# Second block: gate units between gelu units, a shorter gelu, and the low halves of three weight units with the gating norm's affine part on GpSimd

## The reference

```python
proj = h @ w_in[l]                       # h (256, 1024), w_in (1024, 4296)
q, ckv, qi, ki, wi, u, v, ga, gb = jnp.split(proj, splits, axis=-1)
...
def chunked_gmlp(u, v, ln_g, ln_b, w_s, b_s):
    u = jax.nn.gelu(u)
    v = layer_norm_2(jax.nn.gelu(v), ln_g, ln_b)
...
    s = jnp.einsum('gij,bcjge->bcige', ws, vc) + jnp.transpose(b_s)[None, None, :, :, None]
...
...
merged = jax.nn.sigmoid(ga) * y_a + jax.nn.sigmoid(gb) * y_b
```

## Time and profile before

| | us |
|---|---|
| median of 3 runs | 1447.15 |
| lowest to highest | 1446.86 to 1449.07 |
| the profiled execution | 1444.45 |
| its span in the trace | 1442.7 |

### The profile page before, as it was taken

One profiled execution on the slowest core, in us unless ns is written; L12 is line 12 of the kernel. 1 busy time (PEld: TensorE's weight loads), 2 busy tenths in 40 slices (PEclk: granted clock), 3 DMA queues, 4 the chain that ended last, 5 costly groups with the idle time before them and its releaser, 6 DMA issues.

```text
span 1442.7 us, 23198 instructions
## 1 busy us (share of the span) xinstructions
PE 1329.4 (92%) x9534; PEld 1157.1 (80%) x9534; DVE 871.0 (60%) x1390; ACT 600.1 (42%) x959; POOL 33.0 (2%) x51
## 2 busy tenths in 40 slices
PE   7999989799999899998989999779799869999995
PEld 6999889698898799987979988678688756666663
DVE  3999867755555699985866455656874642222213
ACT  4346663444444434666444444434353322212211
POOL 1000000000000000000000000020040000000000
PEclk9999999999999999999999999989999979999998
DMA  9754435365555464442546555464346539999980
GB/s 287 252 177 144 141 89 162 130 232 184 176 193 184 135 227 150 147 132 88 189 151 199 178 200 175 139 198 140 118 140 234 208 139 399 406 397 418 414 335 31
DMA packets 172295, 289.97 MB, mean 201 GB/s; under 512 B 10292, under 2 KB 143044, under 8 KB 159916
## 3 DMA queue, kind: packets, MB, share of 16 engines
q1 hardware_dynamic: 169292, 281.55, 55.8%
q0 software_dynamic: 2752, 7.07, 1.7%
q10 hardware_dynamic: 160, 0.08, 0.0%
HBM read 287.61 MB, written 3.16 MB: 202 GB/s over the span
## 4 chain that ended last, share of the span: by engine, by line
PE 65%; DVE 26%; ACT 5%; issue 3%; DMA 1%; DVEq 0%; SPq 0%; ACTq 0%
PE ps L1536 15%; PE ps L1537 15%; PE ps L1538 15%; DVE w_lo L991 8%; PE ps L1929 8%; DVE cvh L1109 5%; PE ps L1956 4%; ACT w_hi L627 3%; PE ps L1913 2%; PE ps L1965 2%; DVE nm L1067 1%; DVE x_nat L1040 1%; DVE gT L1032 1%; DVE ro L1101 1%; DVE ps L1066 1%
## 5 line engine op out<-in xcount | busy, mean ns | idle before, releaser
L991 DVE TENSOR_TENSOR w_lo<-raw,w_hi 128x2048 fp32r<-128x2048 f32 (+1 forms) x170 | 378.4, 2226 | 175.9 <-ACT w_hi L627 175.8
L627 ACT ACTIVATE w_hi<-raw 128x2048 fp32r<-128x2048 f32 (+1 forms) x170 | 316.8, 1863 | 265.1 <-PE ps L1538 258.7
L1536 PE MATMUL ps<-xT_hi,w_lo 128*128 128x256 f32 (+1 forms) x1224 | 356.6, 291 | 9.8 <-DVE xT_lo L1009 7.2
L1537 PE MATMUL ps<-xT_lo,w_hi 128*128 128x256 f32 (+1 forms) x1224 | 349.5, 286 | 0.0
L1538 PE MATMUL ps<-xT_hi,w_hi 128*128 128x256 f32 (+1 forms) x1224 | 348.9, 285 | 0.0
L1536 PEld LDWEIGHTS ps<-xT_hi,w_lo 128*128 128x128 f32 (+1 forms) x1224 | 236.8, 194 | 21.0 <-issue 11.9
L1537 PEld LDWEIGHTS ps<-xT_lo,w_hi 128*128 128x128 f32 (+1 forms) x1224 | 237.2, 194 | 0.5
L1538 PEld LDWEIGHTS ps<-xT_hi,w_hi 128*128 128x128 f32 (+1 forms) x1224 | 237.0, 194 | 0.2
L1536 PE MATMUL ps<-w_hi,xT_lo 128*128 128x256 f32 (+2 forms) x560 | 171.2, 306 | 2.0 <-DVE w_lo L991 1.7
L1537 PE MATMUL ps<-w_lo,xT_hi 128*128 128x256 f32 (+2 forms) x560 | 168.5, 301 | 0.0
L1538 PE MATMUL ps<-w_hi,xT_hi 128*128 128x256 f32 (+2 forms) x560 | 168.4, 301 | 0.0
(11 more groups left out here) (363 smaller groups left out, 1894.5 us busy)
## 6 DMA issues: line engine op xcount, KB each, us to landing
raw<-in_w_in SPq DMA_DIRECT2D x72, 1024.0 KB, 5.1
raw<-in_w_ff SPq DMA_DIRECT2D x64, 1024.0 KB, 5.2
raw<-in_w_gate SPq DMA_DIRECT2D x10, 1024.0 KB, 7.2
raw<-in_w_up SPq DMA_DIRECT2D x10, 1024.0 KB, 8.9
w_exp<-in_w_down SPq DMA_DIRECT2D x10, 1024.0 KB, 9.8
raw<-in_w_o SPq DMA_DIRECT2D x8, 1024.0 KB, 4.8
w_exp<-in_w_gate SPq DMA_DIRECT2D x8, 1024.0 KB, 8.8
raw<-in_w_down SPq DMA_DIRECT2D x8, 1024.0 KB, 10.3
```

What stands on the lines that cost most here:

```text
L627: nc.scalar.activation(w_hi[:, u % SPLIT, 0:n], raw[:, u % RAW, 0:n], ACT.Copy).then_inc(hi_done, 1)
L991: nc.vector.tensor_tensor(w_lo[:, u % SPLIT, 0:n], raw[:, u % RAW, 0:n], w_hi[:, u % SPLIT, 0:n].bitcast(F32), ALU.subtract).then_inc(spli ...
L1536: nc.tensor.matmul(out_, left[1], right[0], start=start, stop=False)
L1537: nc.tensor.matmul(out_, left[0], right[1], start=False, stop=False)
```

## The change

Four things change, all in the stretch of units 5 to 12 of the second block:

- W_V is 5 and W_U is now 8; X_LNV stays 8. The columns of the units 7 and 9 change places in kind: v is 5 and 6 as before, the first gate unit is 7, u is 8 and 9, the other gates are 10 to 16.
- The gelu's polynomial is one DVE instruction instead of two; the constant goes into ACT's tanh scale.
- The low halves of units 8, 9 and 10 are made on GpSimd. DVE keeps the counting: after `small(w, 1)` of w = 7, 8 and 9 it waits for GpSimd's low half of unit w+1 and increments `split_done`. (Where DVE made them, it did so at w = 6, 7 and 8.)
- The gain and bias of the gating norm go to GpSimd too, behind the three low halves; the statistics move from w = 7 to w = 8, ahead of that unit's gelu. The top-key parts run at w = 5, 6, 7 and 9, 10, 11, between the polynomial and the result of a gelu unit.

```diff
+GELU_AT = (W_V, W_V + 1, W_U, W_U + 1)
+GATE_AT = (7, 10, 11, 12, 13, 14, 15, 16)
+POOL_LO = (8, 9, 10)
+TOP_AT = {5: (0, 0), 6: (0, 1), 7: (0, 2), 9: (1, 0), 10: (1, 1), 11: (1, 2)}
...
             bias_load(0)
+            for w in POOL_LO:
+                u = G2 + w
+                pool.wait_ge(hi_done, u + 1)
+                nc.gpsimd.tensor_tensor(w_lo[:, u % SPLIT, :], raw[:, u % RAW, :], w_hi[:, u % SPLIT, :].bitcast(F32), ALU.subtract).then_inc(pool_lo, 1)
+
+            pool.wait_ge(lnv_hat, 1)
+            nc.gpsimd.tensor_tensor(vg, vg, bc(lnv_g, 1, TT), ALU.mult).then_inc(lnv_gain, 1)
+            pool.wait_ge(lnv_gain, 1)
+            nc.gpsimd.tensor_tensor(vg, vg, bc(lnv_b, 1, TT), ALU.add).then_inc(lnv_out, 1)
...
                 small(w, 0)
                 small(w, 1)
-                split2(G2 + w + 2, W_COLS.get(w + 2, UCOLS))
-                if W_V <= w < W_GA:
-                    n = w - W_V
-                    dve.wait_ge(ev2, w + 1)
-                    then(nc.vector.tensor_scalar(gel_s, gel_s, 0.044715, 1.0, ALU.mult, ALU.add))
-                    nc.vector.tensor_tensor(gel_s, gel_s, gel_x, ALU.mult).then_inc(gel_poly, 1)
...
-                if w == W_U:
+                if w + 1 in POOL_LO:
+                    dve.wait_ge(pool_lo, POOL_LO.index(w + 1) + 1)
+                    dve.sem_inc(split_done, 1)
+                if w + 2 not in POOL_LO:
+                    split2(G2 + w + 2, W_COLS.get(w + 2, UCOLS))
+                if w == X_LNV:
...
-                if w == X_LNV:
-                    dve.wait_ge(lnv_hat, 1)
-                    then(nc.vector.tensor_tensor(vg, vg, bc(lnv_g, 1, TT), ALU.mult))
-                    nc.vector.tensor_tensor(vg, vg, bc(lnv_b, 1, TT), ALU.add).then_inc(lnv_out, 1)
-                if 0 <= w - X_TOP < 6:
-                    top_keys((w - X_TOP) // 3, (w - X_TOP) % 3)
+                if w in GELU_AT:
+                    n = GELU_AT.index(w)
+                    dve.wait_ge(ev2, w + 1)
+                    nc.vector.scalar_tensor_tensor(out=gel_s, in0=gel_s, scalar=1.0 / 0.044715, in1=gel_x, op0=ALU.add, op1=ALU.mult).then_inc(gel_poly, 1)
+                if w in TOP_AT:
+                    top_keys(*TOP_AT[w])
+                if w in GELU_AT:
...
```

More of the change, by code:

```diff
@@ L497, in _ @@
             load2(W_K, w2[:, :, O_KI:O_KI + 72], KC, K_COLS, KV_RANK, 72)
-            for w0, o, n in ((W_Q, O_Q, 2), (W_V, O_V, 2), (W_U, O_U, 2), (W_GA, O_GA, 4), (W_GB, O_GB, 4)):
-                for j in range(n):
-                    load2(w0 + j, w2[:, :, o + 256 * j:o + 256 * (j + 1)], KC, 256)
+            col_of = {W_Q + j: O_Q + 256 * j for j in range(2)}
+            col_of.update({w: o for w, o in zip(GELU_AT, (O_V, O_V + 256, O_U, O_U + 256))})
+            col_of.update({w: O_GA + 256 * g for g, w in enumerate(GATE_AT)})
+            for w in range(W_Q, W_PB):
+                load2(w, w2[:, :, col_of[w]:col_of[w] + 256], KC, 256)
             for w0, name in ((W_PB, "w_proj_b_2"), (W_PA, "w_proj_a_2")):
@@ L875, in _ @@
                     act.wait_ge(gel_poly, n + 1)
-                    nc.scalar.activation(gel_s, gel_s, ACT.Tanh, scale=2.0 * GELU_C).then_inc(gel_th, 1)
+                    nc.scalar.activation(gel_s, gel_s, ACT.Tanh, scale=2.0 * GELU_C * 0.044715).then_inc(gel_th, 1)
                 else:
-                    g = 2 * (w - W_GA)
+                    g = 2 * GATE_AT.index(w)
                     nc.scalar.activation(gT[:, g:g + 2, :], two, ACT.Tanh, scale=0.5).then_inc(ev2, 1)
@@ L1359, in _ @@
                     nc.vector.scalar_tensor_tensor(out=nmr[:], in0=mv[:, :, 0], scalar=-1.0, in1=nw[:, 1, 0:TT], op0=ALU.mult, op1=ALU.mult).then_inc(lnv_stat, 1)
-                if w == X_LNV:
-                    dve.wait_ge(lnv_hat, 1)
-                    then(nc.vector.tensor_tensor(vg, vg, bc(lnv_g, 1, TT), ALU.mult))
-                    nc.vector.tensor_tensor(vg, vg, bc(lnv_b, 1, TT), ALU.add).then_inc(lnv_out, 1)
-                if 0 <= w - X_TOP < 6:
-                    top_keys((w - X_TOP) // 3, (w - X_TOP) % 3)
+                if w in GELU_AT:
+                    n = GELU_AT.index(w)
+                    dve.wait_ge(ev2, w + 1)
[3 more added lines that the diff above has]
+                if w in GELU_AT:
+                    dst = (vg, ug)[n // 2][:, :, 256 * (n % 2):256 * (n % 2) + 256]
+                    dve.wait_ge(gel_th, n + 1)
+                    nc.vector.scalar_tensor_tensor(out=dst, in0=gel_s.rearrange("p (a c) -> p a c", a=TT), scalar=1.0,
+                                                   in1=gel_x.rearrange("p (a c) -> p a c", a=TT), op0=ALU.add, op1=ALU.mult).then_inc(gel_out, 1)
                 if w == X_SP:
```

18 lines of the change are left out of this document (7 added, 11 removed).

## The result

| | before | changed |
|---|---|---|
| median | 1446.92 us (8 runs) | 1451.58 us (8 runs) |
| lowest to highest | 1443.47 to 1449.26 | 1449.15 to 1455.11 |
| the profiled execution | 1444.45 | 1450.38 |
| its span | 1442.7 | 1448.5 |

Ratio 1.0042, with a 95% interval of 1.0028 to 1.0055: slower, by 4.7 us of the medians. (The ratios in this document are those on record. So the direction is certain and the size of the first comparison is at the small end.

The account below looks back on a forecast made before the run. DVE was taken to bound units 7 to 12, PE the rest; unit 8 late by 11.2 us, plus 2 of slow clock, less what DVE's relief wins back, gave +9.5 on 1447.15: 1456.6 us, range 1443 to 1461.5.

Parts of the forecast that it names:

- The engines exclude each other on long instructions: Units 7 to 12: DVE and GpSimd take turns at 2048 elements too, giving DVE rows of 3 to 5 us.
- The list of what is held: DVE's index additions, gelu instructions and low halves, with two SBUF inputs, are held; maxima, replacements and PSUM reads are not.
- The first rival: Engines overlap on long instructions, so the low halves are free: about 1440 us, faster; chance 0.18.
- A low half on GpSimd takes 4.5 us: GpSimd's low halves of units 8 to 10: 4.5 us each, bounds 4.3 and 5.9; gain and bias 2.4 each.
- The second rival: GpSimd takes pieces and lets DVE in between, a half lasting some 9 us: -2, 1445 us; chance 0.08.
- Its other branch: Unit 7's index pair gets in ahead of GpSimd's half of unit 9: +5, 1452 us; within the forecast's 0.74.
- Unit 8 starts +11.2 us: PE starts unit 8 at 1014.6 instead of 1003.4, its count standing behind an index pair that GpSimd holds.
- Slow clock behind the pause, 2 us: After some 11 us of standing before unit 8, PE runs slow and loses 1.4 to 3 us, taken as 2.
- The additions behind the spatial products +10, unit 17 +9.5: DVE's additions come at 1052.4 instead of 1042.3; a wait shortened by about 0.5 then leaves +9.5 us.
- ACT's gelu waits as long as before: ACT's tanh waits for DVE's gelu polynomial, 15.2 us in the kernel before, stay as long.
- Order and gelu by themselves nothing: Units 5 to 12: the order of columns by itself was priced at nothing, with the same loads and PE matmuls.
- The sum's own bounds: Whole kernel: +6.5 us with no clock loss and 4.3 us halves, to +15 with 5.9 us halves; 1453.5 to 1462.

Follow-up runs that it names:

- the repeat: The changed kernel run once more with no edit: 1454.13 us against 1444.67 for the kernel before, ratio 1.0064.
- experiment 1: Kernel before plus three two-input GpSimd subtractions of 128 x 2048 that no engine waits for: 1451.42 us against 1443.65, ratio 1.0061.
- Experiment 2: Kernel before plus nine GpSimd fills, which only write, three in a row at three places: 1447.0 us against 1443.65, ratio 1.0021.
- experiment 4: Changed kernel with one more wait ahead of each low half on GpSimd, so it asks later: 1445.94 us against 1443.65 for the kernel before, ratio 1.0002.
- experiment 6: Changed kernel with DVE's wait and count for units 8 to 10 ahead of the index additions: 1444.88 us against 1444.67 for the kernel before, ratio 0.9995.
- experiment 7: Kernel before with only the gelu's polynomial in one DVE instruction: 1442.97 us, ratio 0.9992.
- experiment 8: Changed kernel with low halves, gain and bias all on DVE, order, statistics and shorter gelu kept: 1444.28 us, ratio 0.9998 to the kernel before.
- experiment 3: Changed kernel with the three low halves back on DVE, everything else kept: 1444.03 us against 1443.65 for the kernel before, ratio 0.9996.
- experiment 9: Changed kernel, low halves on DVE, polynomial ahead of norm statistics, norm applied after unit 9's latent copy: 1441.26 us against 1444.39 for the kernel before, ratio 0.9983.

## Why the prediction was right

The forecast was slower, 1456.6 us in 1443.0 to 1461.5; measured were 1451.58 and, the second time, 1454.13. The mechanism is the one forecast, and each of its steps has a row:

- **The engines exclude each other on long instructions.** The rows before showed it at 256 elements a partition; carried to 2048 it holds: 4.69, 4.6 and 4.21 us on two index additions and unit 8's polynomial, where 3 to 5 were forecast. The list of what is held was too short: it names instructions with two inputs, and experiments 1, 2, 4 and 6 show `tensor_scalar` with one input held as well. In the changed kernel none of the three long holds is on such an instruction. The first rival (1440 us) needed additions of 0.5 us; experiment 1 refutes it by itself.
- **A low half on GpSimd takes 4.5 us.** 4.79, 4.52 and 4.58, the first with 0.3 us of waiting for DVE in it; gain and bias 2.34 and 2.38 where 2.4 were forecast. The second rival's rows of 7 us or more don't occur, so its middle way (1445 us) did not happen. Its other branch, an index addition slipping in ahead of GpSimd, did not happen either, but experiment 4 made something like it by hand, at all three places, and the stretch was +1.6 us over the kernel before where that branch, at one place, had been put at +5.
- **Unit 8 starts +11.2 us.** It started at 1013.16, +9.8, 1.4 us earlier than in the sum. More than half of this, 0.8, is the first hold: GpSimd got in between the two additions of a pair, so only the held one was left behind it, 0.3 us, where I had priced the whole pair at 1.1. From there to GpSimd's second half it took 4.2 us instead of 4.5, and from that half's end to unit 8 0.9 instead of 1.2. The second hold fell where the sum had it, ahead of the last pair.
- **Slow clock behind the pause, 2 us.** The granted clock was 0.55 for 6 us, and unit 8's first half took 5.4 us to the latent product (1013.16 to 1018.51). At full clock the matmuls of the next half follow each other every 0.12 us, so 24 of them take 2.9: the cost was 2.5.
- **The additions behind the spatial products +10, unit 17 +9.5.** They came at 1050.73, +8.4, and unit 17 at 1108.89, +9.1 by the clock of the trace, +9.4 by the stretch. So between the two the delay grew by 0.7 where the sum had it shrink by 0.5, and the agreement at unit 17 is closer than its terms: 1.4 us too much ahead of unit 8 and 1.2 too little at the end nearly cancel. That is luck. The 0.7 is clock. PE's wait for the attention (line 380, 375 before) ends 13.3 us behind the additions in both kernels; in the 5 us behind it the granted clock was 0.50 in both profiles of the changed kernel and 0.66 in both of the kernel before, and unit 17 comes 44.8 and 44.1 us later.
- **ACT's gelu waits as long as before**: 14.2 us in sum against 15.2.
- **Order and gelu by themselves nothing**: experiments 7 and 8, 0.7 us either way.

**What was off is the sum against the median.** I carried the +9.5 of unit 17 unchanged to the end. The profiled execution grew by 5.9 and the median by 4.7; the repeat grew by 9.5. The sum's own bounds were +6.5 to +15 (1453.5 to 1462), so the first comparison lies below them and only the repeat inside. It is the wider range of the chances, stretched down to 1443 to take in part of the first rival, that holds 1451.58. That the second rival's other branch had named 1452 is chance, since what it describes did not happen. The noise was read too small as well: from three executions, 0.15% apart, I took 0.2% as the least that can be told from nothing, and the eight of the comparison lie 0.4% apart. In the profiles 2.9 of the missing 3.3 us are in two places behind unit 17. One is PE's granted clock after the wait of 2.71 us there. Before, and in the changed kernel:

```profile
1100.00:1105.00 5.00, 5.00 (x31) 5.00 (x31) 1.51 (x1) 0.00 (x0) 0.00 (x0) 0.66 0.98 412
```

```profile
1109.00:1114.00 5.00, 5.00 (x43) 5.00 (x44) 1.62 (x1) 0.00 (x0) 0.00 (x0) 1.00 1.00 415
```

The kernel before runs its first us of unit 17 partly at the lower level (0.66) and the changed one at full clock: from unit 17 to a load issued four units on it is 27.5 us and 26.0. The other is the end, from the issue of the last store to the last instruction, 5.7 us and 4.3.

**What stays open** is whether these two are chance. Both profiles of the kernel before show 27.4 to 27.5 and 5.7, both of the changed kernel 26.0 and 4.3. Other kernels mix them: the shorter gelu alone has 26.0 and 4.7, the low halves on DVE 27.3 and 4.3. So neither hangs on the low halves, but with two profiles each I can't say that a kernel has no fixed value. The first of the two does go with the clock in all thirteen profiles: 26.0 us in the five with a granted clock of 1.00 in the 5 us behind the wait, 27.3 to 27.5 in the seven with 0.66 to 0.73, and 28.6 in the one with 0.50 (experiment 4), though the wait is 2.71 us in each. It may hang on the clock in the stretch: the four profiles with 0.50 behind the wait on line 380 (the changed kernel twice, the count moved, the shorter gelu alone) all have 1.00 behind unit 17's. The medians say that a part is chance: that of the kernel before was 1446.92 in the first comparison and between 1443.65 and 1444.67 in the four others, and the changed one had 1451.58 and 1454.13. Of the 4.8 us between the two comparisons of the changed kernel (+4.7 and +9.5) 2.3 are thus the kernel before and 2.5 the changed one. No run tried to tell it apart further. A second thing is open: what of the 4.5 us that the low halves cost with the count moved (experiment 6 against 3) is DVE's holds and what is GpSimd's 4.5 us against DVE's 2.3 on the path; both stand on the same path and no run took one without the other.

## What to carry to other kernels

Before work is given to GpSimd because it is idle, look at the instructions that DVE will run at that time: two SBUF inputs on both sides means that they take turns, and a one-input `tensor_scalar` of DVE is no way out, so a low half of 2.3 us taken off DVE came back as a hold of up to 4.7 us on it. Look for an old row in which the two touch, however short, and read which of them got longer; here three short contacts foretold the whole. And where a semaphore must be raised by an in-order engine on behalf of another, put it ahead of anything that the other can hold: that alone was worth 6.6 us of the stretch. When a wait goes, ask what is late next: experiment 9 removed a wait of 5.1 us for 0.9, and it took one more move to be paid.

## What the runs showed of the hardware that I had not expected

- Fills on GpSimd, which read nothing, leave DVE's two-input instructions alone (2290 and 484 ns) but hold its one-input `tensor_scalar` of 128 x 512 (421 ns alone, 1038 in the mean of four, 1.77 us at the longest). Experiment 2 shows it.
- Very small one-input instructions are caught too. With the count moved (experiment 6), the first step of the norm's root, on two elements a partition, took 3.08 us while GpSimd made its third low half; and in experiment 4 a `tensor_scalar` of 128 x 128 took 4.45 us; without a hold the two take 0.17 and 0.29. The row of experiment 6:

```profile
1016.84 3.08 DVE L1368 TENSOR_SCALAR nw<-mv 128x2 f32<-128x2 f32 x1
```

- GpSimd's subtraction of 128 x 2048 took 3.60 us where both inputs were the same tile (experiment 1), and 4.52 to 4.79 with two tiles and the output type that the low half has. Which of the two differences does it was not tried.
- After waits of the same length (2.71 us) at the same place PE's granted clock was 0.66 for the next 5 us in the kernel before and 1.00 in the changed one, each seen twice, and 0.50 in that of experiment 4. What decides it is open.
